# A gate projection from seven block products instead of eight, and a transposed scatter in alternating row halves

## The reference, cut to what matters

```python
def rmsnorm(x, g):
    y = x * lax.rsqrt(jnp.mean(x * x, axis=-1, keepdims=True) + EPS)
    return y * g

x = x + moe_swiglu(rmsnorm(x, g_ffn), ...)                         # 32 experts, top 4 of 32
ple_gate = jax.nn.sigmoid(rmsnorm(x, g_ple_gate) @ w_ple_gate)     # (256 x 1024) @ (1024 x 1024)
ple = rmsnorm(p @ w_ple_proj, g_ple_post)
x = x + ple_gate * ple
```

## Time and profile before

| | us |
|---|---|
| median of 3 runs | 1175.84 |
| lowest, highest | 1175.23, 1176.26 |
| profiled execution, its own time | 1173.45 |
| its span | 1171.7 |
| mean granted TensorE clock | 0.999 of full speed |

### The profile page before, as it was taken

The page is one execution under the profiler, slowest core; times in us unless marked ns, Lnnn a source line. Parts: engine busy times, 40 slices in busy tenths (PEclk is TensorE's granted clock), DMA queues, the critical chain, the costliest instruction groups (busy, mean ns, idle before and its releaser), DMA issues.

```text
span 1171.7 us, 15747 instructions
## 1 busy us (share of the span) xinstructions
PE 1112.1 (95%) x6546; PEld 499.6 (43%) x6546; DVE 394.3 (34%) x845; ACT 172.9 (15%) x268; POOL 138.7 (12%) x163
## 2 busy tenths in 40 slices
PE   8999999999999999999999999999999999998998
PEld 4588787533333333333333333333333333333344
DVE  6547859442222222222132222222223222222222
ACT  2262012320000000000211111111111111111111
POOL 2995654300000000000000000000000000000000
PEclk9999999999999999999999999999999999999999
DMA  9932447799999999999999999999999999999981
GB/s 309 344 126 72 144 154 290 312 419 428 427 428 435 426 436 430 427 436 432 426 433 434 427 436 432 424 436 433 427 434 430 430 437 432 425 435 424 427 360 37
DMA packets 40047, 441.04 MB, mean 376 GB/s; under 512 B 9748, under 2 KB 10064, under 8 KB 22352
## 3 DMA queue, kind: packets, MB, share of 16 engines
q1 hardware_dynamic: 38800, 436.91, 88.7%
q0 software_dynamic: 1104, 3.67, 0.9%
q10 hardware_dynamic: 112, 0.02, 0.0%
HBM read 439.54 MB, written 1.05 MB: 376 GB/s over the span
## 4 chain that ended last, share of the span: by engine, by line
PE 80%; DMA 12%; DVE 5%; ACT 2%; issue 1%; SPq 0%; DVEq 0%
PE bank L1693 32%; PE bank L1748 17%; DMA ring<-in_w_up_dram 8%; PE bank L1373 7%; PE bank L1763 5%; PE bank L1388 4%; DMA ring<-in_w_down_dram 3%; PE bank L1857 2%; PE bank L1533 2%; PE bank L1569 2%; PE bank L1541 2%; PE bank L1730 2%; DVE arena L1201 2%; DVE arena L1205 2%; DVE arena L1199 2%; ACT arena L798 1%
## 5 line engine op out<-in xcount | busy, mean ns | idle before, releaser
L1693 PE MATMUL bank<-ring,arena 128*64 128x512 f32 x2048 | 447.8, 594 | 5.6 <-DMA ring<-in_w_up_dram 5.5
L1693 PEld LDWEIGHTS bank<-ring,arena 128*64 128x64 f32 x2048 | 143.7, 137 | 304.3 <-issue 293.0
L1748 PE MATMUL bank<-ring,arena 128*64 128x512 f32 x1024 | 228.5, 599 | 16.9 <-ACT arena L798 14.8
L1223 DVE TENSOR_TENSOR arena<-arena,bank 128x512 f32<-128x512 f32 x128 | 79.5, 682 | 286.6 <-PE bank L1763 286.4
L1748 PEld LDWEIGHTS bank<-ring,arena 128*64 128x64 f32 x1024 | 72.3, 137 | 152.4 <-issue 140.5
L1197 DVE TENSOR_SCALAR arena<-bank 128x512 f32<-128x512 f32 x32 | 22.1, 692 | 333.6 <-PE bank L1693 333.6
L796 ACT ACTIVATE arena<-arena 128x512 f32<-128x512 f32 x32 | 20.2, 631 | 476.1 <-DVE arena L1197 476.1
L1373 PE MATMUL bank<-arena,ring 128*128 128x256 f32 x384 | 86.4, 382 | 0.0
L1373 PEld LDWEIGHTS bank<-arena,ring 128*128 128x128 f32 x384 | 71.8, 190 | 12.7 <-issue 3.5
L1763 PE MATMUL bank<-arena 64*128 64x512 f32 x256 | 64.4, 615 | 0.0
L1667 PEld LDWEIGHTS bank<-arena 128*128 128x128 bf16 x1488 | 45.1, 98 | 25.2 <-issue 25.2
(11 more groups left out here) (266 smaller groups left out, 768.8 us busy)
## 6 DMA issues: line engine op xcount, KB each, us to landing
ring<-in_w_up_dram SPq DMA_DIRECT2D x40, 4096.0 KB, 24.7
ring<-in_w_down_dram SPq DMA_DIRECT2D x24, 4096.0 KB, 26.7
ring<-in_w_up_dram SPq DMA_DIRECT2D x45, 2048.0 KB, 17.3
ring<-in_w_down_dram SPq DMA_DIRECT2D x15, 2048.0 KB, 13.7
ring<-in_w_in_dram SPq DMA_DIRECT2D x7, 2048.0 KB, 15.7
ring<-in_w_up_dram SPq DMA_DIRECT2D x6, 1024.0 KB, 33.0
ring<-in_w_glu_dram SPq DMA_DIRECT2D x2, 2048.0 KB, 8.4
ring<-in_w_out_dram SPq DMA_DIRECT2D x2, 2048.0 KB, 7.8
```

The lines of the kernel that those rows point to most:

```text
L1223: dve.tensor_tensor(part, part, bank[at][:, :], ALU.add).then_inc(m["sc_add"], 1)
L1693: last = pe.matmul(bank[UG + w][HALF * h:HALF * (h + 1), :].rearrange("p (m j) -> p m j", j=4), XS[:, k, :], columns[:, h, :, :], start=Fa ...
L1748: last = pe.matmul(bank[YB][HALF * c:HALF * (c + 1), :], ACTT[:, j, HALF * h:HALF * (h + 1)], piece[:, j, 512 * c:512 * (c + 1)], start=(h ...
```

## The change

The product of the 256x1024 rows with the 1024x1024 weights is written as a product of 2x2 blocks, each block of rows 128 tokens by 512, each block of weights 512 by 512. Eight block products of four 128x512 matmuls become seven (Winograd's form). For that, four sums of weight blocks are formed on GpSimd (`GW_SUM`, each 128x2048 elements: L631, L634, L635 and L637 of the changed kernel), and four sums of row blocks on DVE (`GM_SUM`, each 128x512). Some products share a bank: a later product adds to an earlier one. ACT copies intermediate values out of PSUM (`keep`, four of 128x512), DVE adds them to others (`pg_sum`, five), ACT takes the sigmoid from SBUF, and DVE's last two steps are as before. `GSIG` and `X3_SQ` move to another ring place. The order of the five output pieces changes. A path for crowded experts keeps the eight products.

The transposed scatter takes its blocks in the order 0, 4, 1, 5, 2, 6, 3, 7.

```diff
             def scatter_turned():
-                for i in range(4):
-                    for k in (2 * i, 2 * i + 1):
...
+                for k in (0, 4, 1, 5, 2, 6, 3, 7):
...
+                    if k % 2:
+                        last.then_inc(S["xt3_full"], 1)
```

GpSimd, at the end of its instructions:

```diff
+            for c in range(2):
+                pool.wait_ge(READ[c], E)
+            pool.wait_ge(arrived[GATE_AT[0]], 16 * LOAD[E, 0])
+            pool.tensor_tensor(GW_SUM[0], gate_weights(0, 1), gate_weights(0, 0), ALU.subtract).then_inc(S["gw_sum"], 1)
+            pool.wait_ge(S["gw_sum"], 1)
+            pool.wait_ge(arrived[GATE_AT[1]], 16 * LOAD[E, 1])
+            pool.tensor_tensor(GW_SUM[1], gate_weights(1, 1), GW_SUM[0], ALU.subtract).then_inc(S["gw_sum"], 1)
+            pool.tensor_tensor(GW_SUM[2], gate_weights(1, 1), gate_weights(0, 1), ALU.subtract).then_inc(S["gw_sum"], 1)
+            pool.wait_ge(S["gw_sum"], 2)
+            pool.tensor_tensor(GW_SUM[3], gate_weights(1, 0), GW_SUM[1], ALU.subtract).then_inc(S["gw_sum"], 1)
```

ScalarE:

```diff
+            def keep(i, full_by, at):
+                act.wait_ge(S["gp_full"], full_by)
+                act.activation(KEPT[i], bank[at][:, :], ACT.Copy).then_inc(S["gp_read"], 1)
+            def gated(i):
+                t, cols = FIRST_PARTS[i]
+                act.wait_ge(S["pg_sum"], i + 1)
+                act.activation(GSIG[:, t, cols], GSIG[:, t, cols], ACT.Sigmoid,
+                               scale=RSTD[:, 4 + t:5 + t]).then_inc(S["pg_sig"], 1)
+            squares(0)
+            keep(0, 1, GX)
             gated(0)
+            keep(1, 3, 7)
+            keep(2, 4, GX)
+            gated(1)
+            keep(3, 6, GX)
+            for i in (2, 3, 4):
+                gated(i)
```

VectorE:

```diff
+            dve.wait_ge(S["xt3_late"], 2)
+            dve.wait_ge(S["xt3_set"], 2)
+            dve.tensor_tensor(GM_SUM[0], gate_rows(0, 1), gate_rows(1, 1), ALU.add).then_inc(S["gm_sum"], 1)
+            dve.wait_ge(S["gm_sum"], 1)
+            dve.tensor_tensor(GM_SUM[1], GM_SUM[0], gate_rows(0, 0), ALU.subtract).then_inc(S["gm_sum"], 1)
+            roots(0)
+            dve.wait_ge(S["gm_sum"], 2)
+            dve.tensor_tensor(GM_SUM[3], gate_rows(1, 0), GM_SUM[1], ALU.subtract).then_inc(S["gm_sum"], 1)
+            dve.tensor_tensor(GM_SUM[2], gate_rows(0, 0), gate_rows(0, 1), ALU.subtract).then_inc(S["gm_sum"], 1)
+            dve.wait_ge(S["gp_read"], 1)
+            dve.wait_ge(S["gp_full"], 2)
+            dve.tensor_tensor(GSIG[:, 0, 0:512], bank[6][:, :], KEPT[0], ALU.add).then_inc(S["pg_sum"], 1)
+            finish(0, *FIRST_PARTS[0])
...
+            dve.wait_ge(S["gp_read"], 4)
+            dve.tensor_tensor(GSIG[:, 1, 512:], KEPT[1], KEPT[3], ALU.add).then_inc(S["pg_sum"], 1)
+            finish(2, *FIRST_PARTS[2])
+            for h in range(2):
...
+                dve.wait_ge(S["gp_full"], 7 + h)
+                dve.tensor_tensor(GSIG[:, 1, cols], bank[(UG, UU)[h]][:, 0:256], KEPT[3][:, cols], ALU.add).then_inc(S["pg_sum"], 1)
+                finish(3 + h, *FIRST_PARTS[3 + h])
```

TensorE; the prediction counts the products P1 to P7 in this order:

```diff
+            gate_product(GX, gate_rows(0, 0), gate_weights(0, 0), (2, 3)).then_inc(S["gp_full"], 1)
...
+            gate_product(6, gate_rows(1, 0), gate_weights(1, 0), start=True).then_inc(S["gp_full"], 1)
+            pe.wait_ge(S["gm_sum"], 1)
+            pe.wait_ge(S["gw_sum"], 1)
+            gate_product(7, GM_SUM[0], GW_SUM[0], start=True).then_inc(S["gp_full"], 1)
+            pe.wait_ge(S["gp_read"], 1)
+            pe.wait_ge(S["gm_sum"], 2)
+            pe.wait_ge(S["gw_sum"], 2)
+            gate_product(GX, GM_SUM[1], GW_SUM[1]).then_inc(S["gp_full"], 1)
+            pe.wait_ge(S["gp_read"], 2)
+            pe.wait_ge(S["gm_sum"], 3)
+            gate_product(7, GM_SUM[3], gate_weights(1, 1)).then_inc(S["gp_full"], 1)
+            pe.wait_ge(S["gp_read"], 3)
+            pe.wait_ge(S["gm_sum"], 4)
+            pe.wait_ge(S["gw_sum"], 3)
+            gate_product(GX, GM_SUM[2], GW_SUM[2]).then_inc(S["gp_full"], 1)
+            pe.wait_ge(S["gw_sum"], 4)
+            for h in range(2):
+                gate_product((UG, UU)[h], gate_rows(1, 1), GW_SUM[3], start=True,
```

More of the change, by code:

```diff
@@ L523, in store @@
             def store(run):
-                for i, (t, cols, _) in enumerate(PARTS):
+                for i, (t, cols) in enumerate((FIRST_PARTS, [part[0:2] for part in PARTS])[run]):
                     sp.wait_ge(S["fin_set"], len(PARTS) * run + i + 1)
@@ L819, in _, with squares @@
                 last.then_inc(S["xt3_late"], 1)
-            def gated(run):
+            def squares(run):
                 for t in range(TB):
@@ L838, in _ @@
                         expert(M, E + e * PASSES + j)
-                gated(1)
+                squares(1)
+                for i, (t, cols, at) in enumerate(PARTS):
+                    act.wait_ge(S["pg_full"], i + 1)
+                    act.activation(GSIG[:, t, cols], bank[at][:, 0:cols.stop - cols.start], ACT.Sigmoid,
+                                   scale=RSTD[:, 4 + t:5 + t]).then_inc(S["pg_sig"], 1)
         @block.vector
@@ L1279, in _, with roots @@
             expert(M, E - 1, True)
-            def finish(run):
+            def roots(run):
                 dve.wait_ge(S["x3_sq"], TB * (run + 1))
@@ L1313, in _ @@
                 turned_rows(range(4)).then_inc(S["xt3_again_set"], 1)
-                finish(1)
+                roots(1)
+                for i, (t, cols, _) in enumerate(PARTS):
+                    finish(len(PARTS) + i, t, cols)
         @block.tensor
@@ L1714, in scatter_turned @@
             def scatter_turned():
-                for i in range(4):
-                    for k in (2 * i, 2 * i + 1):
[L1718 to L1723, removed]
+                for k in (0, 4, 1, 5, 2, 6, 3, 7):
+                    rows = slice(HALF * (k // 4), HALF * (k // 4 + 1))
+                    last = pe.matmul(bank[XT3B[k // 2]][:, SEQ * (k % 2):SEQ * (k % 2 + 1)],
+                                     Y[rows, :].rearrange("p (m k) -> p k m", k=4)[:, k % 4, :],
+                                     WSELT[rows, :, :].rearrange("p t n -> p (t n)"), start=False, stop=True,
+                                     skip_group_check=True)
+                    if k % 2:
+                        last.then_inc(S["xt3_full"], 1)
             def down(m, n, piece_in, bias_of_next=True):
@@ L1869, in gates, with gate_product @@
                     gate(part, range(DT))
-            gates()
+            def gate_product(at, of, w, ks=range(4), start=False, cols=slice(0, 512)):
+                b = bank[at][:, 0:cols.stop - cols.start]
+                for k in ks:
+                    last = pe.matmul(b, of[:, k, :], w[:, k, cols], start=start and k == 0, stop=(k == 3), skip_group_check=True)
+                return last
+            pe.wait_ge(S["xt3_set"], 1)
+            pe.wait_ge(arrived[GATE_AT[0]], 16 * LOAD[E, 0])
+            gate_product(GX, gate_rows(0, 0), gate_weights(0, 0), (0, 1), start=True)
+            pe.wait_ge(S["xt3_late"], 1)
+            gate_product(GX, gate_rows(0, 0), gate_weights(0, 0), (2, 3)).then_inc(S["gp_full"], 1)
+            pe.wait_ge(S["xt3_set"], 2)
+            pe.wait_ge(S["xt3_late"], 2)
+            pe.wait_ge(arrived[GATE_AT[1]], 16 * LOAD[E, 1])
+            gate_product(6, gate_rows(1, 0), gate_weights(1, 0), start=True).then_inc(S["gp_full"], 1)
[16 more added lines that the diff above has]
+                gate_product((UG, UU)[h], gate_rows(1, 1), GW_SUM[3], start=True,
+                             cols=slice(256 * h, 256 * (h + 1))).then_inc(S["gp_full"], 1)
             with pe.If(crowd > CAP):
```

47 lines of the change are left out of this document (24 added, 23 removed).

## The result

| | before | changed |
|---|---|---|
| median of 10 runs each, us | 1175.71 | 1181.05 |
| lowest, highest | 1173.06, 1176.29 | 1176.99, 1182.0 |
| profiled execution, its own time | 1173.45 | 1181.5 |
| its span | 1171.7 | 1179.5 |
| mean granted TensorE clock | 0.999 | 0.993 |

The changed kernel is slower: ratio 1.0045, 95% interval 1.0036 to 1.0054, or 5.3 us on 1175.71. The two profiled executions differ by 8.05 us, more than the medians, because that of before was 2.3 us faster than its median and that of the changed kernel 0.45 slower. So the profile tells where the time is, and the timed runs how much it is. Eight of the ten runs took 1180.4 to 1182.0, two took 1177.0 and 1177.7.

A forecast was written before the change was run, and what follows sets the result against it. TensorE bounds the end before; in the changed kernel, VectorE's sums held by GpSimd. VectorE's end 3.6 us later (3.8 in the other draw), taken as +3.7 on 1175.84, gives 1179.5; own range 1178.5 to 1180.7, whole range 1174.5 to 1181.6.

The forecast's parts named there:

- the forecast's chain: Fifth product waits for bank 7's copy, behind the first sigmoid and all four sums of rows; TensorE idles 6 us.
- rival C: The 128x2 scaling of the sums of squares is held by GpSimd too: +4.2 or +5.3 us, chance 0.14.
- GpSimd first: GpSimd's second weight sum precedes VectorE's first sum of rows; GpSimd ends at 1155.25, the sums of rows at 1156.4.
- The products alone: Seven block products, from their start to VectorE's end: 28.0 us instead of 29.1, if nothing waits.
- The scatter: Transposed scatter in alternating row halves saves 1.3 us (bounds 0 and 1.6), swallowed by the wait at the fifth product.
- The landing: The second gate piece arrives at 1140.8; GpSimd's last three weight sums cannot start before.
- The end behind the sixth product: Copy, sum, sigmoid, multiplication and additions after the sixth product take 7.2 us; the seventh hides beneath.
- VectorE held by GpSimd: A VectorE instruction with two SBUF operands waits for a whole GpSimd sum, then gets in before the next.
- Rival A: VectorE and GpSimd do not hold each other here: 2.4 us less, 1173.4; chance 0.10.
- rival B: Two sums of rows pass before GpSimd's second weight sum, fifth product at 1153.5: 1174.5 us, chance 0.16.
- The draw: Whether VectorE's first sum of rows (1140.7) or GpSimd's second weight sum (1140.8) goes first: within 0.1 us, open.
- P1 to P4 find their operands: The first four of the seven block products were claimed to find their operands, at no cost.

The follow-up runs named there:

- the products alone: The changed kernel with the transposed scatter back in its old order: ratio 1.0053 to the kernel before, median 1180.84 us.
- the narrow scaling: The changed kernel with the 128x2 scaling of the sums of squares as two instructions of 128x1: ratio 1.0033 to the kernel before, median 1179.21 us.
- narrow again: Second run of the changed kernel with the scaling as two 128x1 instructions, beside the changed kernel on one chip: ratio 1.0031 to the kernel before, median 1177.63 us.
- the scatter alone: The kernel before with only the transposed scatter in alternating row halves: ratio 0.9989 to the kernel before, median 1173.53 us.
- changed again: Second run of the unaltered changed kernel, beside its variants on one chip: ratio 1.0049 to the kernel before, median 1181.37 us.
- the copy's order alone: The changed kernel with the copy of bank 7 ahead of the first sigmoid, scaling still 128x2: ratio 1.0045 to the kernel before, median 1180.9 us.
- both edits: The changed kernel with two 128x1 scalings and the copy of bank 7 ahead of the first sigmoid: ratio 0.9998 to the kernel before, median 1175.5 us.
- the filled wait: The changed kernel with seven more matmuls into an unused bank before the wait for the fourth product: ratio 1.0036 to the kernel before, median 1178.63 us.

## Why the prediction was right or wrong

**Right in direction and within the whole range, 1.5 us short** (1179.5 against 1181.05), but above the forecast's own range (1178.5 to 1180.7), and not by the forecast's chain: what came is rival C with GpSimd first, 1181.1, which had a chance of 0.14. And it is in part luck. From profile to profile, as the sum was made, it gave +3.7 against a measured +8.05; a held instruction and a fallen clock were missing, and the step from the profile to the median made up for most of it. By its steps:

- The products alone, 28.0 us from the first product to VectorE's end: 28.01 in the two kernels with this end in which nothing waits.
- The scatter, 1.3 us: 1.1. That its gain is swallowed by the wait: so, by the products alone.
- The landing at 1140.8: 1140.7. GpSimd's second sum with no VectorE sum let in 4.51, those behind it 4.94 (forecast 4.91).
- The end behind the sixth product, 7.2 us: 7.14.
- VectorE held by GpSimd, one instruction each: so. Rival A is refuted by the two held sums, and rival B was never seen.
- **The step that failed** is the one that chose between the forecast and rival C: that the scaling of 128x2 isn't held. It was put at nothing in the forecast without a row to rest on: the one row near it, 128x32 with a GpSimd instruction just ending, decided nothing, as the prediction says itself. It took 4.45. So the place of the wait was wrong, before P4 and not before P5. For C with GpSimd first the prediction gave P4 at 1156.6; it started at 1156.17. With the narrow scaling the forecast's own chain came true from P5 on, within 0.2 us. The Trainium skill, VectorE: DVE Perf Modes, section Mode 2×_2P, says that a tensor_scalar with source and destination in SBUF can use both read ports, each reading one half of the tensor, if the dimension that is split, the outermost that isn't 1, is even (or odd and equal in both). Read so, two elements per partition suffice and one can't be split. The trace agrees: 4.45 for 128x2, 0.20 for two of 128x1. No run here shows the ports themselves.
- **The draw** was taken as even. In the eight profiles of kernels with all four sums on GpSimd, GpSimd's second sum went ahead of VectorE's first each time, by 0.2 to 0.3 us in three and by 1.2 to 2.8 in the other five, in which the scatter began at 1137.0 to 1137.6 instead of 1135.2 and the second sum still between 1140.3 and 1141.6. It made no difference to P4, which stood 15.47 to 15.51 behind GpSimd's second sum in all five with the wide scaling. The prediction's "P1 to P4 find their operands" holds only with VectorE first: by its own sum the second sum of rows ends at 1150.9 with GpSimd first, behind P4's 1149.0, and narrow again shows that wait, 2.34 us. It costs nothing while P5 waits longer.
- **The term that was missing**: the clock, 2.9 us in the profiled execution. The forecast had TensorE idle for 6 us too, and counted that time and not what it does to the products behind. VectorE's end by C with GpSimd first is 1169.10 + 5.3 = 1174.4; with P4 0.4 earlier than it said and 2.9 for the clock that is 1176.9, and 1176.73 was measured.
- **The step from the profile to the median.** The sum was made against 1173.45 and then moved up by 2.4, as if both kernels came later in a common execution. But the end of the changed kernel hangs on the landing: its two profiles have the scatter at 1135.15 and 1137.37, and VectorE's end at 1176.73 and 1176.63. A kernel in which nothing waits ends with its scatter instead: from the scatter's start to VectorE's end it is 34.20 us before and 33.09 with the scatter alone, 1.1 apart like the scatter itself, though the scatter began at 1134.90 in one and 1136.60 in the other. A later scatter, as in many of these profiles, would make before slower and the changed kernel not. That would be why 5.3 us in the medians stand beside 8.05 in the profiles, and the missing clock and this step would nearly cancel. It is argued and not shown, since before has one profile, with an early scatter.

**What stays open**: the two runs of the changed kernel at 1177. They aren't alone: changed again has two of six at 1178.3 and 1178.6, the copy's order alone two of eight at 1176.1 and 1176.9. By the numbers above VectorE first would bring 1.1 us (+4.2 instead of +5.3) and a clock that held 2.8, so only both together reach 1177; this is an estimate, and no profile caught such an execution. The clock by itself doesn't tell them apart: with the copy's order alone its mean was 0.997 both at 1176.1 and at 1181.2. Nor is it shown why the clock held through a wait of 2.47 us in one execution and fell during one of 2.34 in another. And of small instructions only 128x2 and 128x1 were tried, no other even or odd width.

## What to carry to other kernels

Before work is put on GpSimd beside VectorE, list every VectorE instruction that will meet it, the smallest too: each with two SBUF operands, and even a scaling of two elements per partition, can cost up to a whole GpSimd instruction and everything queued behind it. If the sum of both engines' work fits on VectorE (here 3 x 2.28 us more), keep it there. And price an idle stretch of TensorE twice: for its length, and for the products behind it, which may run at half the clock.

## What the runs showed of the hardware that I had not expected

- A VectorE TENSOR_SCALAR on 128x2 float32 takes 0.16 us alone and 4.45 beside a GpSimd sum; two on 128x1 take 0.20 there. Not every instruction with one SBUF source is held: the RECIPROCAL of 128x2 takes 0.17 in the middle of such a sum.
- A sum of 128x2048 float32 takes GpSimd 4.5 us and VectorE 2.28; while they hold each other, a GpSimd sum takes 4.9, and a VectorE instruction up to as long as a GpSimd one (4.87 for a sum of 128x512 that takes 0.69 alone).
- The clock fell to half in five profiles with waits of 2.34 to 6.56 us before P4: in four of them during the wait (in the changed kernel 2.1 us after the last product), in the products alone 1.0 us after work had resumed behind a wait of 4.13. It was full again at about 1155.3 in narrow again and between 1161.1 and 1162 in the other four, in the changed kernel 6 us after work had resumed. It held through waits of 1.36 us (both edits) and 2.47 (narrow scaling). Against the 14.02 of the filled wait, the last four products lost 1.7 (products alone), 2.6 (changed again, copy alone) and 2.8 us (changed).
- Matmuls of 64 rows that alternate between the row halves take 2.24 us per 16 with strided operands, and the four ordinary ones behind them start 2.05 after the first. In the old order, one half after the other, the eight matmuls cost 1.1 us more.
